# One copy of turned weights, zero rows under the query remainders, and leading parts first behind the norms

## The chip, the core and the metric

The kernel runs on one core of a Trainium2 chip. The metric is the device time of one launch in microseconds; before the change its median over three runs is 1998.62 us (1998.11 to 2001.07). The engines are named as in the profile: PE is TensorE (PEld its weight loads), DVE is VectorE, ACT is ScalarE, POOL is GpSimd, SP is SyncE, which issues the loads of weights.

## What is computed

Three transformer blocks over 512 tokens of width 1024, in float32 accuracy. The first has windowed attention (12 heads, 128 keys to either side, one learned sink logit per head), the second neighbourhood attention on a grid of 8 columns, both beside four heads that attend to 256 memory rows, and both with a gated MLP. The third has two attentions side by side, a dilated one (12 heads) and a stick-breaking one (8 heads), and an MLP with a squared ReLU. Every block begins with an RMS norm. What matters here:

```
h = rms_norm(x, g);  proj = h @ w                 # at each block and before each MLP
p = softmax(concat([q k^T / 8 + bias, sink]));  o = p[:, :keys] @ v
z = q k^T / 8
log_a = log_sigmoid(z) + suffix_sum(log_sigmoid(-z))   # stick-breaking, strictly causal
o_b = where(causal, exp(log_a), 0) @ v
```

## The kernel before

Activations lie turned: a tensor `[128, 8, 512]` holds 8 chunks of 128 features by 512 tokens. To keep float32 accuracy at the fast matmul rate, every weight and activation is split in a leading part (`w_hi`, `h_hi`, rounded) and a remainder (`w_lo`, `h_lo`), and each product is three matmuls of 128 rows and 512 columns: leading by leading, leading weight by remainder of the activation, remainder of the weight by leading activation. ACT makes the leading parts (L542 for weights, `lead`, L588, for activations), DVE the remainders (L943, and `trail`, L965). Weights come in units of 512 KB into a ring of four; a load waits until the unit four before it is used up.

The order on each engine is written out by hand, and all hand-overs are semaphores.

**The norms.** Behind each attention and each MLP of the first two blocks stands `add_normed` on DVE: for each chunk `scale` (times the norm's root, L977 or L979), `add` (into `xT`, L990), and `trail`. ACT turns each new chunk of `xT` into `h_hi`. The order is scale 0, add 0, and then per chunk scale c+1, trail c, add c+1. PE meanwhile runs `keep_busy` (3 and 16 idle matmuls) and then the first three tiles of the next stage in "stairs": `first_chunks` for chunk 0, and then per chunk c all three matmuls of tile 0, of tile 1, and of tile 2 at chunk c-2, after waiting for the remainder `h_lo` of chunk c. The stage `proj[0]` at the very start of the kernel has the same stairs, behind 12 warm-up matmuls.

**The softmax stages.** `softmax` runs over steps, each a pair of heads (on partition rows 0 to 63 and 64 to 127) and 128 queries: phase 0 has 24 window steps and 8 memory steps, phase 1 has 24 grid and 8 memory steps, phase 2 is the dilated attention. In iteration s PE makes the scores of step s (L1562), multiplies the values of step s-3 (L1602) and turns the weights of step s-2 (L1629). DVE adds the bias and finds the maximum of s (L1040) and divides step s-1 by its sum (L1062); ACT copies the turned weights of s-2 from PSUM (`copy_turned`, L653, one copy for each head), takes the exponentials of s (L665) and copies a finished pair's output (L676), whose remainder DVE takes at the end of the same iteration (L1073). In phase 0 each step also has a matmul of one column of zeros for each head (L1569), which leaves a zero in PSUM to which the sink is added as a bias.

**The stick-breaking stage.** For each head PE makes scores z into three PSUM banks (leading by leading, with the key's remainder in the other 64 rows, L1769; then the query's remainder over 64 rows, L1771; then a mask, L1777), the first half of a gate tile (L1424), the triangular sums of the head before (L1793, L1800) and the gate tile's second half. Every second head the values of a pair follow the scores (L1752). DVE reads the gate tile from its bank (L1246) before the next may start in it.

Of the kernel before, what the change touches and what calls it, by code (L numbers as in the profile page):

```python
# [8 lines left out]
P = 128  # L9
D = 1024  # L10
S = 512
DC = D // P
HD = 64
MEM = 256
# [25 lines left out]
def program(nc, t, out):  # L40
# [49 lines left out]
    with ExitStack() as ctx:  # L90
# [186 lines left out]
        class Step:  # L277


            def __init__(self, pair, pair_no, qtile, pieces, vs, biased, blocks=None, key_rows=None):  # L280
# [3 lines left out]
                self.width = sum(both[0]["width"] for both in pieces)  # L284
                self.blocks = blocks or [(first, P) for first in range(0, pieces[0][0]["keys"], P)]
# [3 lines left out]
                for p in pieces[0]:  # L289
                    if "scores" not in p:  # L290
                        p["scores"] = [(slice(0, P), p["first_key"], p["keys"], p["q"], p["k"])]
# [4 lines left out]
        def mem_steps(layer):  # L296
            steps = []
            for c in range(2):
                for i in range(4):
                    both = [dict(q=q_buf[rows(half), 6 + c, P * i:P * i + P], k=mk[rows(half), layer, c, :],  # L300
                                 bias=zero_bias[:, :], width=MEM, keys=MEM, first_key=0, sink=None, at=0)
# [6 lines left out]
        def window_steps():  # L308
            steps = []
            for c in range(6):  # L310
                for i in range(4):
                    lo_t, hi_t = max(0, i - 1), min(3, i + 1)
                    keys = P * (hi_t - lo_t + 1)
                    if hi_t == i + 1:
                        b0, first_key, sink = 1 + P * (lo_t - i + 1), 0, keys
                    else:
                        b0, first_key, sink = 0, 1, 0
                    both, vs = [], []
                    for half in range(2):
# [4 lines left out]
                                         first_key=first_key, sink=sink, at=0))  # L324
# [4 lines left out]
        def grid_steps():  # L329
# [5 lines left out]
            for c in range(6):  # L335
                for i, (k0, keys, b0, blocks, tiles, key_rows) in enumerate(spans):
                    both = [dict(q=q_buf[rows(half), c, P * i:P * i + P], k=k_buf[rows(half), c, k0:k0 + keys],
                                 bias=bias_grid[:, 2 * (c % 2) + half, b0:b0 + keys], width=keys, keys=keys,
                                 first_key=0, sink=None, at=0) for half in range(2)]
# [5 lines left out]
        def dilated_steps():  # L345

            steps = []
            for p in range(2):
                for i in range(4):
# [5 lines left out]
                    for half in range(2):  # L355
# [5 lines left out]
                        for g in (1, 2):  # L361
                            c = 2 * g + p
                            for r in range(4):
# [7 lines left out]
                                         keys=width, first_key=0, sink=None, at=0))  # L371
# [158 lines left out]
        def _(act):  # L530
# [115 lines left out]
            def copy_turned(phase, d, steps):  # L646
                if d >= 2:
                    act.wait_ge(pv_done, pv[0] + d - 1)
                for half in range(2):
# [58 lines left out]
            for c in range(DC):  # L708
                if c < 3:
                    hi_to(c)  # L710
# [223 lines left out]
        def _(dve):  # L934
# [33 lines left out]
            def add_normed(n, f, at_, f_side, post, pre, turned_layer=None):  # L968
# [44 lines left out]
            def softmax(phase, o_hi, o_lo, beside=None, read=None, last_values=None):  # L1013
                steps = attention[phase]
                n = len(steps)
                if last_values:
                    lo_to(last_values[0] + 3)
                for s in range(n + S_LAG_V):
                    if s == 2 and last_values:
                        values([last_values])  # L1020
                    if s < n:
                        st = steps[s]
                        if s >= 3:
                            dve.wait_ge(t_ready, turned[0] + sum(2 * len(x.pieces) for x in steps[:s - 2]))
                        for k, both in enumerate(st.pieces):
                            for half, p in enumerate(both):
# [9 lines left out]
                                if k:  # L1036
# [5 lines left out]
                                    in0=bank_in(phase, masked[0] % 4)[:, :p["width"]], in1=p["bias"], scale=-1.0,  # L1042
# [20 lines left out]
                    d = s - S_LAG_V  # L1063
                    if 0 <= d < n and steps[d].last:
                        st = steps[d]
                        o_count[0] += 1
                        dve.wait_ge(o_hi_done, o_count[0])
                        dst, src = o_lo[:, st.pair, :], bank_in(phase, 6 + st.pair_no % 2)[:, :]
                        lead = o_hi[:, st.pair, :].bitcast(F32)
                        if phase == 2:  # L1070
                            lead = unclassed(lead, src)[0]
                            dst, src = unclassed(dst, src)
                        nc.vector.tensor_tensor(dst, src, lead, ALU.subtract).then_inc(o_ready, 1)  # L1073
# [4 lines left out]
                turned[0] += sum(2 * len(x.pieces) for x in steps)  # L1078
# [8 lines left out]
            for c in range(DC):  # L1087
                if c < 3:
                    lo_to(c)
                trail(c, xT[:, c, :], h_hi[:, c, :], h_lo[:, c, :], G_MIX_PRE)  # L1090
# [115 lines left out]
            nc.vector.tensor_copy(ident_r[:, :], ident[:, :]).then_inc(masks_rounded, 1)  # L1206
            softmax(2, o2_hi, o2_lo, proj_sb, read_qk(range(4), lambda k: sb_q[k] if k < 4 else sb_k[k - 4]))
# [98 lines left out]
        def _(pe):  # L1306
# [29 lines left out]
            def chunk_order(st):  # L1336
# [7 lines left out]
                stairs = []  # L1344
                for c in range(1, DC):
                    stairs += [(0, 0, c), (1, 0, c)]
                    if c >= 2:
                        stairs += [(2, 0, c - 2)]
                return stairs + [(2, 0, DC - 2), (2, 0, DC - 1)] + [(k, 0, c) for k in range(3, len(st.tiles)) for c in range(DC)]

            def first_chunks(st, rhs, wait_rhs):

                (u0, _, _), (u1, _, _) = st.tiles[0][0], st.tiles[1][0]
                hi, lo = rhs(0)
                acc0, acc1 = bank_of(st, side[0], 0)[:, :], bank_of(st, side[0], 1)[:, :]
                cols = slice(0, P)
                pe.wait_ge(h_hi_done, n_h[0] - DC + 1)
                pe.wait_ge(w_hi_done, u0 + 1)
                mm(acc0, w_hi[:, u0 % 4, cols], hi, start=True, stop=False)
                pe.wait_ge(w_split, u0 + 1)  # L1360
                mm(acc0, w_lo[:, u0 % 4, cols], hi, start=False, stop=False)
                if u0 == 0:
                    wait_rhs(0)
                    mm(acc0, w_hi[:, u0 % 4, cols], lo, start=False, stop=False)
# [607 lines left out]
```

## Time and profile before

| | |
|---|---|
| median of three runs | 1998.62 us |
| the profiled execution | 2001.56 us, span 1999.8 us |
| PE busy | 1961.0 us (98%) |
| DVE busy | 964.6 us (48%) |
| ACT busy | 784.9 us (39%) |
| mean granted clock of PE | 0.994 |

The span runs from the first to the last instruction of the profiled execution; its own time is 1.76 us more. A busy share of PE of 98% says that PE hardly ever stood still, not that each matmul ran as fast as it can: the time between the starts of neighbouring matmuls is what tells that.

### The profile page before, as it was taken

The page shows a single profiled execution, that of the slowest core. Times are in us where ns is not written, and L with a number is a line of the kernel's source. Part 1 is how long each engine was busy: PE and PEld are TensorE (multiplying, and loading weights), DVE is VectorE, ACT ScalarE, POOL GpSimd, SP SyncE. Part 2 cuts the span into 40 slices and gives each one's busy share as a digit, 9 for nine tenths or more (in the row PEclk, how much of TensorE's full clock was granted, in tenths as well). Part 3 has the DMA queues.
Part 4 walks back from the last instruction along what each step waited for, and adds up shares of the span by engine and source line. Part 5 has one row for each costly group of instructions (what it writes and reads, how often), then busy time and mean ns, then how long its engine had stood idle before and what let it go on. Part 6 is the DMA issues. An engine that isn't in the chain of part 4 may idle for free.

```text
span 1999.8 us, 24785 instructions
## 1 busy us (share of the span) xinstructions
PE 1961.0 (98%) x10258; PEld 1594.3 (80%) x10258; DVE 964.6 (48%) x1461; ACT 784.9 (39%) x1315; POOL 163.7 (8%) x182
## 2 busy tenths in 40 slices
PE   9999999999999999999999999999999999999997
PEld 7976788888887866788888887988777888888886
DVE  4675465554226365465554227343554556424532
ACT  5376433333323276533333324233763443212321
POOL 3110210000004030220000002000000010000000
PEclk9999999999999999999999999999999999999999
DMA  5420233333332320233333333331202333333322
GB/s 179 140 65 24 62 115 95 95 97 97 96 100 91 95 62 24 64 106 101 99 95 92 97 99 104 95 107 49 69 30 66 106 95 96 101 99 95 95 95 84
DMA packets 51975, 178.75 MB, mean 89 GB/s; under 512 B 6364, under 2 KB 7772, under 8 KB 51736
## 3 DMA queue, kind: packets, MB, share of 16 engines
q1 hardware_dynamic: 49512, 169.14, 27.3%
q0 software_dynamic: 2208, 7.97, 1.5%
q8 instruction: 82, 1.34, 0.3%
q14 instruction: 29, 0.24, 0.0%
q10 hardware_dynamic: 144, 0.06, 0.0%
HBM read 174.48 MB, written 2.66 MB: 89 GB/s over the span
## 4 chain that ended last, share of the span: by engine, by line
PE 92%; ACT 3%; DVE 3%; issue 1%; DMA 1%; SPq 0%; DVEq 0%; ACTq 0%
PE bank L1405 24%; PE bank L1407 24%; PE bank L1406 24%; PE bank L1602 2%; PE bank L1629 2%; PE bank L1424 2%; PE bank L1562 2%; PE bank L1426 1%; PE bank L1425 1%; PE bank L1465 1%; PE bank L1464 1%; PE bank L1463 1%; ACT prob_short L665 1%; ACT pt_short L653 1%; PE bank L1793 1%
## 5 line engine op out<-in xcount | busy, mean ns | idle before, releaser
L943 DVE TENSOR_TENSOR w_lo<-w_raw,w_hi 128x1024 fp32r<-128x1024 f32 (+1 forms) x326 | 401.1, 1232 | 747.1 <-ACT w_hi L542 746.9
L1405 PE MATMUL bank<-h_hi,w_hi 128*128 128x512 f32 x1402 | 553.9, 395 | 6.6 <-DVE h_lo L965 6.4
L542 ACT CAST w_hi<-w_raw 128x1024 fp32r<-128x1024 f32 (+1 forms) x326 | 329.4, 1011 | 588.2 <-DMA w_raw<-in_w_down 133.1
L1406 PE MATMUL bank<-h_lo,w_hi 128*128 128x512 f32 x1402 | 547.0, 390 | 0.0
L1407 PE MATMUL bank<-h_hi,w_lo 128*128 128x512 f32 x1402 | 547.0, 390 | 0.0
L1405 PEld LDWEIGHTS bank<-h_hi,w_hi 128*128 128x128 f32 x1402 | 263.8, 188 | 73.2 <-DVE h_lo L965 15.8
L1407 PEld LDWEIGHTS bank<-h_hi,w_lo 128*128 128x128 f32 x1402 | 263.9, 188 | 55.7
L1406 PEld LDWEIGHTS bank<-h_lo,w_hi 128*128 128x128 f32 x1402 | 263.9, 188 | 55.4 <-issue 1.9
L1405 PE MATMUL bank<-a_hi,w_hi 128*128 128x512 f32 (+1 forms) x752 | 290.6, 386 | 0.0
L1407 PE MATMUL bank<-a_hi,w_lo 128*128 128x512 f32 (+1 forms) x752 | 289.2, 385 | 0.0
L1406 PE MATMUL bank<-a_lo,w_hi 128*128 128x512 f32 (+1 forms) x752 | 289.1, 385 | 0.0
L1405 PEld LDWEIGHTS bank<-a_hi,w_hi 128*128 128x128 f32 x752 | 141.3, 188 | 29.0 <-issue 0.9
L1406 PEld LDWEIGHTS bank<-a_lo,w_hi 128*128 128x128 f32 x752 | 141.3, 188 | 28.8 <-issue 0.7
L1407 PEld LDWEIGHTS bank<-a_hi,w_lo 128*128 128x128 f32 x752 | 141.3, 188 | 28.1
L446 POOL COPY sq_sum<-sq 128x512 f32<-128x512 f32 x6 | 3.8, 626 | 1099.7 <-ACT sq L584 1099.7
L665 ACT ACTIVATE prob_short<-prob_short,low_stat 128x256 f32<-128x256 f32 (+6 forms) x144 | 74.9, 527 | 24.1 <-DVE low_stat L1040 24.1
L759 ACT CAST a_hi<-raw 128x512 fp32r<-128x512 f32 x44 | 27.3, 621 | 125.6 <-DVE raw L1140 125.6
L449 POOL TENSOR_TENSOR sq_sum<-sq_sum,sq 128x512 f32<-128x512 f32 x36 | 49.9, 1385 | 282.4 <-ACT sq L584 282.4
L756 ACT ACTIVATE act_out<-act_out 128x512 f32<-128x512 f32 x44 | 27.8, 633 | 95.0 <-DVE act_out L1135 95.0
L1629 PE MATMUL bank<-ident,prob_short 128*128 128x128 f32 (+3 forms) x340 | 52.5, 283 | 6.7 <-DVE prob_short L1062 5.5
L653 ACT ACTIVATE pt_short<-bank 128x256 f32<-128x256 f32 (+1 forms) x128 | 44.9, 405 | 28.0 <-PE bank L1629 28.0
L1424 PE MATMUL bank<-h_hi,w_hi 128*128 128x512 f32 x128 | 53.2, 416 | 2.0 <-DVE gate_sb L1246 1.1
(219 smaller groups left out, 2213.8 us busy)
## 6 DMA issues: line engine op xcount, KB each, us to landing
w_raw<-in_w_gu SPq DMA_DIRECT2D x88, 512.0 KB, 3.5
w_raw<-in_w_mlp_in SPq DMA_DIRECT2D x32, 512.0 KB, 3.5
w_raw<-in_w_mlp_out SPq DMA_DIRECT2D x32, 512.0 KB, 3.6
w_raw<-in_w_down SPq DMA_DIRECT2D x32, 448.0 KB, 3.3
w_raw<-in_w_out SPq DMA_DIRECT2D x24, 512.0 KB, 3.6
w_raw<-in_w_down SPq DMA_DIRECT2D x16, 512.0 KB, 3.5
w_raw<-in_w_gates SPq DMA_DIRECT2D x16, 512.0 KB, 3.5
w_raw<-in_w_qk_b SPq DMA_DIRECT2D x14, 512.0 KB, 3.5
```

Source lines behind the costliest of these rows:

```text
L449: made = nc.gpsimd.tensor_tensor(sq_sum[:, :], sq_sum[:, :], sq[:, c % 2, :], ALU.add)
L542: nc.scalar.copy(slot(w_hi, v), slot(w_raw, v)).then_inc(w_hi_done, 1)
L653: nc.scalar.activation(buf[:, :w], bank_in(phase, 4 + turned[0] % 2)[:, :w], ACT.Copy).then_inc(pt_copied, 1)
L665: nc.scalar.activation(part, part, ACT.Exp, bias=top, scale=-1.0, accum_out=sums[:, s % 4, half, k:k + 1]).then_inc(p_exp, 1)
L943: nc.vector.tensor_tensor(slot(w_lo, v), slot(w_raw, v), slot(w_hi, v).bitcast(F32), ALU.subtract).then_inc(w_split, 1)
L1405: mm(acc, w1, hi, start=start, stop=False)
L1406: mm(acc, w1, lo, start=False, stop=False)
L1407: last = mm(acc, w2, hi, start=False, stop=end)
L1424: mm(ps[7][:, :], w1, hi, start=c == 0, stop=False)
L1562: last = mm(bank_in(phase, (scored[0] + half) % 4)[of, first:first + w], q, k, start=True, stop=True)
L1602: last = mm(out_, v, turned_p, start=x == 0, stop=x == n_v - 1, skip_group_check=phase == 2)
L1629: last = nc.tensor.transpose(bank_in(phase, 4 + turned[0] % 2)[:w, P * kt:P * kt + P], prob_of(phase, d, half)[:, at_ + first:at_ + first ...
```

## The change

1. Window steps keep the scores where the bias has its columns (`col`), so that the sink's zero stays in one of two fixed columns of each score bank. Eight matmuls of one column of zeros ahead of phase 0 write those columns once; the two in every step go.
2. Steps with two blocks of keys (in phase 0 the first and last query tile of a pair and all memory steps, in phase 1 all steps) turn both heads' weights into one PSUM bank, and ACT makes one copy of 512 columns in place of two of 256. Steps with three blocks and phase 2 keep two copies.
3. In phases 0 and 1 DVE takes an output's remainder one iteration later, between the maximum of step s and the division of step s-1.
4. Behind the norms DVE goes scale 0, add 0, scale 1, add 1, and then per chunk trail c, scale c+2, add c+2. PE first multiplies the leading activation of chunk c (tiles 0 and 1), then all of tile 2 at chunk c-2, and only then waits for `h_lo` of chunk c. `keep_busy` has 14 matmuls for 16. At the start of the kernel there are 16 warm-up matmuls for 12, and the second and third weight unit are split one chunk of activations later.
5. The query's remainder of the stick-breaking scores is multiplied over 128 rows, the other 64 of which DVE has set to zero ahead of phase 2.

```diff
+                if steps[d].copies == 1:
+                    both = pt_short[:, 2 * (d % 2):2 * (d % 2) + 2, :2 * P]
+                    act.wait_ge(t_ready, turned[0] + 1)
+                    nc.scalar.activation(both, bank_in(phase, 4 + turned[0] % 2)[:, :].rearrange("p (h q) -> p h q", h=2),
+                                         ACT.Copy).then_inc(pt_copied, 1)
...
-                if c < 3:
-                    hi_to(c)
+                if c in (0, 2, 3):
+                    hi_to(max(0, c - 1))
...
-                scale(0)
-                add(0)
+                for c in range(2):
+                    scale(c)
+                    add(c)
                 for c in range(DC):
-                    if c + 1 < DC:
-                        scale(c + 1)
                     trail(c, xT[:, c, :], h_hi[:, c, :], h_lo[:, c, :], pre)
-                    if c + 1 < DC:
-                        add(c + 1)
+                    if c + 2 < DC:
+                        scale(c + 2)
+                        add(c + 2)
...
+                    if phase < 2:
+                        output_remainder(s - S_LAG_V - 1)
...
+            for half in range(2):
+                none = zero_bias[rows(1 - half), :].rearrange("p (o t) -> p o t", o=1).to_broadcast([HD, 2, MEM])
+                nc.vector.tensor_copy(sb_ql[rows(1 - half), half, :].rearrange("p (o t) -> p o t", o=2),
+                                      none).then_inc(masks_rounded, 1)
...
+                for c in range(done, DC):
+                    pe.wait_ge(h_hi_done, n_h[0] - DC + c + 1)
+                    lead_part(0, c)
+                    lead_part(1, c)
+                    if c >= 2 and c - 2 >= (1 if done else 0):
+                        whole(2, c - 2)
+                    wait_rhs(c)
+                    remainder(0, c)
+                    remainder(1, c)
+                whole(2, DC - 2)
+                whole(2, DC - 1)
...
+                for bank in range(4 if phase == 0 else 0):
+                    for c in (0, 385):
+                        mm(bank_in(0, bank)[:, c:c + 1], q_buf[rows(bank % 2), 0, :P], zero_bias[rows(bank % 2), 0:1], start=True,
+                           stop=True)
...
-                            for half, p in enumerate(both):
-                                if p["sink"] is not None:
-
-                                    mm(bank_in(phase, (scored[0] + half) % 4)[:, p["sink"]:p["sink"] + 1], p["q"],
-                                       zero_bias[rows(half), 0:1], start=True, stop=True).then_inc(s_ready, 1)
...
+                            one, base = steps[d].copies == 1, 2 * P * half if steps[d].copies == 1 else 0
...
-                            last.then_inc(t_ready, 1)
-                            turned[0] += 1
+                            if half or not one:
+                                last.then_inc(t_ready, 1)
+                                turned[0] += 1
...
-                    keep_busy(16, after)
+                    keep_busy(14, after)
...
-                            mm(acc, sb_ks[own, s % 2, keys], sb_ql[own, s % 2, P * kt:], start=False, stop=False,
+                            mm(acc, sb_ks[:, s % 2, keys], sb_ql[:, s % 2, P * kt:], start=False, stop=False,
```

`lead_part` is the two matmuls by `h_hi`, `remainder` the one by `h_lo`, `whole` both. At the kernel's start chunks 0 and 1 of tiles 0 and 1 and chunk 0 of tile 2 come ahead of this loop.

## Rows read from the trace of the kernel before

**Rows 1.** Page, part 4: the chain that ended last, shares of the span

```profile
PE 92%; ACT 3%; DVE 3%; issue 1%; DMA 1%; SPq 0%; DVEq 0%; ACTq 0%
```

**Rows 2.** Waits of PE's weight loads: us in total, times, longest us

```profile
PEld bank L1602 <- ACT pt_short L653: 18.1, 44, 1.0
PEld bank L1405 <- DVE h_lo L965: 15.8, 29, 1.5
```

**Rows 3.** Timeline of a head's stick-breaking scores: start us, us, engine, line, instruction

```profile
1434.50 0.39 PE L1769 MATMUL bank<-sb_qs,sb_ks 128*128 128x512 f32 x1
1434.82 0.50 PE L1771 MATMUL bank<-sb_ql,sb_ks 64*128 64x512 f32 x1
1435.24 0.33 PE L1777 MATMUL bank<-unseen,ident_r 128*128 128x128 f32 x1
...
1437.52 0.45 PE L1424 MATMUL bank<-h_hi,w_hi 128*128 128x512 f32 x1
```

**Rows 4.** Timeline of the triangular sums, full rows throughout

```profile
1429.23 0.39 PE L1793 MATMUL bank<-L_lo,neg_tri 128*128 128x512 f32 x1
1429.46 0.34 PE L1800 MATMUL bank<-L_hi,neg_ones 128*128 128x384 f32 x1
...
1429.81 0.28 PE L1800 MATMUL bank<-L_hi,neg_ones 128*128 128x256 f32 x1
...
1430.05 0.22 PE L1800 MATMUL bank<-L_hi,neg_ones 128*128 128x128 f32 x1
```

**Rows 5.** The gate tile's bank: two timeline rows, and 8 us with clock behind POOL

```profile
1424.75 0.77 PE L1424 MATMUL bank<-h_hi,w_hi 128*128 128x512 f32 x1 [1.05 <-DVE gate_sb L1246]
...
1435.39 0.69 DVE L1246 TENSOR_TENSOR gate_sb<-bank,rstd 128x512 f32<-128x512 f32 x1
...
1420.00:1428.00 8.00, 6.95 (x23) 4.75 (x22) 7.56 (x10) 7.30 (x12) 0.00 (x0) 0.79 0.22 66
```

**Rows 6.** Timeline behind the first norm of block one, DVE and PE

```profile
229.45 0.69 DVE L977 TENSOR_TENSOR f_in_big<-f_in_big,rstd 128x512 f32<-128x512 f32 x1 [3.73 <-ACT rstd L600]
230.18 0.69 DVE L990 TENSOR_TENSOR xT<-xT,f_in_big 128x512 f32<-128x512 f32 x1
230.79 0.68 DVE L977 TENSOR_TENSOR f_in_big<-f_in_big,rstd 128x512 f32<-128x512 f32 x1
...
231.66 0.75 DVE L965 SCALAR_TENSOR_TENSOR h_lo<-xT,gains,h_hi 128x512 fp32r<-128x512 f32 x1 [0.19 <-ACT h_hi L588]
...
231.88 0.47 PE L1359 MATMUL bank<-h_hi,w_hi 128*128 128x512 f32 x1
...
232.33 0.69 DVE L990 TENSOR_TENSOR xT<-xT,f_in_big 128x512 f32<-128x512 f32 x1
...
246.69 0.91 DVE L965 SCALAR_TENSOR_TENSOR h_lo<-xT,gains,h_hi 128x512 fp32r<-128x512 f32 x1 [0.80 <-ACT h_hi L588]
...
251.22 0.39 PE L1405 MATMUL bank<-h_hi,w_hi 128*128 128x512 f32 x1
```

**Rows 7.** Timeline of softmax steps: window, grid, and dilated (the last row)

```profile
127.34 0.28 PE L1569 MATMUL bank<-zero_bias,q_buf 64*128 64x1 f32 x4
127.55 0.66 PE L1602 MATMUL bank<-pt_short,v_buf 128*64 128x128 f32 x8
...
133.00 0.88 PE L1629 MATMUL bank<-ident,prob_short 128*128 128x128 f32 x6 [0.30 <-DVE prob_short L1062]
...
733.56 0.66 PE L1629 MATMUL bank<-ident,prob_short 128*128 128x128 f32 x4
...
734.10 0.66 ACT L653 ACTIVATE pt_short<-bank 128x256 f32<-128x256 f32 x2 [0.33 <-PE bank L1629]
...
734.81 0.81 PE L1602 MATMUL bank<-pt_short,v_buf 128*64 128x128 f32 x8
...
1389.44 1.08 ACT L653 ACTIVATE pt_dil<-bank 128x512 f32<-128x512 f32 x2 [5.25 <-PE bank L1629]
```

**Rows 8.** Timeline at the start of the kernel, PE

```profile
13.22 0.79 PE L1405 MATMUL bank<-h_hi,w_hi 128*128 128x512 f32 x1
```

More of the change, by code:

```diff
@@ L290, in __init__ @@
                     if "scores" not in p:
-                        p["scores"] = [(slice(0, P), p["first_key"], p["keys"], p["q"], p["k"])]
+                        self.copies = 1 if len(self.blocks) == 2 else 2
+                        p["scores"] = [(slice(0, P), p["col"] + p["first_key"], p["keys"], p["q"], p["k"])]
         def rows(half):
@@ L313, in window_steps @@
                     keys = P * (hi_t - lo_t + 1)
[L314 to L317, printed above, removed]
+                    b0, first_key = (1 + P, 0) if i == 0 else (0, 1)
                     both, vs = [], []
@@ L338, in grid_steps @@
                                  bias=bias_grid[:, 2 * (c % 2) + half, b0:b0 + keys], width=keys, keys=keys,
-                                 first_key=0, sink=None, at=0) for half in range(2)]
+                                 first_key=0, col=0, at=0) for half in range(2)]
                     vs = [[v_buf[part, kt, P * c + 64 * half:P * c + 64 * half + 64]
@@ L1017, in softmax, with output_remainder @@
                     lo_to(last_values[0] + 3)
+                def output_remainder(d):
+                    if not (0 <= d < n and steps[d].last):
+                        return
+                    st = steps[d]
+                    o_count[0] += 1
+                    dve.wait_ge(o_hi_done, o_count[0])
+                    dst, src = o_lo[:, st.pair, :], bank_in(phase, 6 + st.pair_no % 2)[:, :]
+                    lead = o_hi[:, st.pair, :].bitcast(F32)
+                    if phase == 2:
+                        lead = unclassed(lead, src)[0]
+                        dst, src = unclassed(dst, src)
+                    nc.vector.tensor_tensor(dst, src, lead, ALU.subtract).then_inc(o_ready, 1)
                 for s in range(n + S_LAG_V):
@@ L1023, in softmax @@
                         if s >= 3:
-                            dve.wait_ge(t_ready, turned[0] + sum(2 * len(x.pieces) for x in steps[:s - 2]))
+                            dve.wait_ge(t_ready, turned[0] + sum(x.copies for x in steps[:s - 2]))
                         for k, both in enumerate(st.pieces):
@@ L1041, in softmax @@
                                     out=prob_of(phase, s, half)[:, p["at"]:p["at"] + p["width"]],
[L1042 removed]
+                                    in0=bank_in(phase, masked[0] % 4)[:, p["col"]:p["col"] + p["width"]], in1=p["bias"], scale=-1.0,
                                     scalar=start, op0=ALU.add, op1=ALU.min,
@@ L1062, in softmax @@
                             nc.vector.tensor_scalar(part, part, rden[:, i, half:half + 1], None, ALU.mult).then_inc(p_ready, 1)
[L1063 to L1073, printed above, removed]
+                    if phase == 2:
+                        output_remainder(s - S_LAG_V)
                     if beside and s < len(beside.tiles) + 1:
@@ L1077, in softmax @@
                         read(s, ps[7], beside.after(s))
-                turned[0] += sum(2 * len(x.pieces) for x in steps)
+                if phase < 2:
+                    output_remainder(n - 1)
+                turned[0] += sum(x.copies for x in steps)
             masked, expd, dens, rdens, o_count, turned = [0], [0], [0], [0], [0], [0]
@@ L1657, in _ @@
             pe.wait_ge(ones_set, 1)
-            for _ in range(12):
+            for _ in range(16):
                 mm(ps[7][:, :P], ones[:, :], ones[:, :], start=True, stop=True)
@@ L1759, in _ @@
                     z = [ps[3 * (s % 2) + b] for b in range(3)]
-                    own = rows(s % 2)
                     if s >= 2:
```

78 lines of the change are left out of this document (42 added, 36 removed).

## The prediction

> **What bounds the kernel now.** First the chain that ended last: 92% of it is PE [rows 1], and PE is busy for nearly the whole span. So a microsecond is won only where PE either waits or issues its matmuls further apart than it could. Next the waits of PE's weight loads: the two largest sums are for ACT's copies of turned weights, 18.1 us in 44 waits, and for `h_lo` behind the norms, 15.8 us in 29 [rows 2]. They are upper bounds, since a load that waits may do so under a running matmul. Last the timeline, for the distances between starts of matmuls, where the page sees nothing: a stretch can be 100% busy and still be slack. All parts of the change touch one of these three, and each is costed in its own stage. Signs: minus is faster.
>
> **Stick-breaking scores.** A head's scores take 1437.52 - 1434.50 = 3.02 us from first start to the next tile [rows 3]. Around the 64-row matmul the starts are 0.32 and 0.42 us apart. Where all matmuls have 128 rows, 512 columns follow each other after 0.23 us, 384 after 0.175 (two in 0.35), 256 after 0.12 (two in 0.24), and for 128 I take half of that, 0.06 [rows 4]. The scores of a head are two each of 512, 384, 256 and 128 columns and masks of 128, 256 and 128: 0.46 + 0.35 + 0.24 + 0.12 + 0.24 = 1.41 us. Saved at full effect 1.61 us a head.
>
> Who is late next? The next gate tile needs its bank read by DVE: that read ended at 1435.39 + 0.69 = 1436.08, while the tile would now start at 1434.50 + 1.41 = 1435.91 [rows 3, 5]. It hangs on the triangular sums before it, so it does not move along; with the hand-over PE waits 0.22. On heads 3, 5 and 7 the values of a pair (over 2 us) stand between and hide this: 3 x 1.61 = 4.83. On heads 2, 4 and 6: 3 x 1.39 = 4.17. On heads 0 and 1 nothing is won: PE already waits 1.05 us for the first bank [rows 5], and that read ends a chain over ACT and DVE (rounding of head 1, absolute values, exponentials, logarithms, split) which does not begin earlier; 3.2 us more of waiting swallow both savings. Sum -9.0.
>
> That longer stand has a price. After the 1.05 us the clock fell to the lower of its two levels, 1.2 GHz, and the 8 us around it show a mean of 0.79 [rows 5], so 0.42 x 8 = 3.4 us at 1.2 GHz (1 is 2.4 GHz, and 0.5 is 1.2 GHz), in part while PE stood. With 4.3 us of standing, more of the slow time falls on matmuls: at most all 3.4 us, which costs 1.7, against about 1.0 now. +0.7, and up to +3 if a second such stretch follows. The Trainium skill (TensorE: Matmul & The Clock Gate, "HAM oscillation — how this bites in real kernels") says that a PE left waiting between bursts is put back to half rate and pays again for warming up. By that rule, too, the stand is not free; it changes none of the terms.
>
> The two DVE writes of zeros come before phase 2, where DVE is idle; a 128x512 pass of such kind is 0.69 [rows 6], so 1.4 us at worst, taken as 0.
>
> **Norms, four times.** Before, DVE's loop is add, ACT's leading part, trail, next add: from the first trail to the eighth (246.69 - 231.66)/7 = 2.15 us a chunk [rows 6]. The eighth ends at 247.60, and then PE still has 15 matmuls: tiles 0, 1 and 2 of the stair's end. The next tile starts at 251.22, 21.77 us after the first scale [rows 6].
>
> After: a dependent add follows its scale after 0.73, an independent instruction an add after 0.61, and a trail is followed after 0.67 [rows 6]. The loop is 0.67 + 0.73 + 0.61 = 2.01 a chunk (2.06 where scale reads PSUM), free of ACT. The first trail starts at 2 x 1.34 = 2.68, the eighth, with nothing but the seventh in front, at about 15.6, and ends at 16.5 with its 0.91. PE has 72 matmuls of 0.23: 16.6 us. It can begin at 2.2 (the first `h_hi`; now 231.88 - 229.45 = 2.43, in part `keep_busy`, whose two matmuls less give that 0.2), waits about 0.3 and 0.6 for the first two remainders, and restarts cost 0.1 each; then nothing stops it: 2.2 + 16.6 + 1.1 = 19.9, or 20.0. Against 21.77: -1.75 a norm. Bounds: PE never waits, 18.8, is -2.9; if DVE keeps its 2.15 a chunk and all trails come 0.7 later, the eighth ends near 18.9, and eight matmuls (1.84) end at 20.8: -0.95. Four norms: -7.0 (-11.6 to -3.8). Behind the stair, weights of its fifth tile are ready early enough: their load hangs on tile 0's end, which moves by some 0.8, and the tile starts 5.5 us after the stair, so little is lost.
>
> **Start of the kernel.** At 13.22 PE has 12 of the stair's 72 matmuls behind it [rows 8]. In the new order it can have 15 by then, since chunk 1 no longer stands behind the second unit's split: 3 x 0.23 = 0.7, and 0.6 for waits of the later chunks and slow clock. The warm-up's four more end about when the first real matmul can start. -1.3 (-2.5 to +0.5).
>
> **Softmax, phases 0 and 1.** In the grid a turn starts at 733.56, ACT's two copies at 734.10, they last 0.66, and the values start at 734.81: 1.25 us, and PE waits for the copy [rows 7]. With one copy ACT may start only when the second head is turned too, two transposes later (0.29), and a 512-column copy lasts 0.60 (two take 1.08 [rows 7], the second starting 0.49 behind the first): 0.54 + 0.29 + 0.60 + 0.05 = 1.48. So the edit that frees ACT lengthens PE's loop: +0.22 a step that has no other wait. Against it, every four steps DVE no longer waits for ACT's output copy; that wait held the turn at 133.00, idle 0.30 and 0.06 of start-up [rows 7], about 0.6 where steps are short.
> - Grid: 6 pairs x (4 x 0.22 - 0.6) = +1.7; memory steps 2 x 0.28 = +0.3 after rounding down for the last. +2.0.
> - Window: the group of zeros costs 127.55 - 127.34 = 0.21 [rows 7], but a switch from 64 to 128 rows then stays exposed for about 0.10. A pair of heads: the step of 256 keys that turned in 1.33 now needs 1.48, and with ACT's queue behind it the next is 0.27 later in all; the other one-copy step wins 0.07, the three-block step 0.16, the wait gone 0.36: -0.35 a pair, -2.1, and +0.5 for the memory steps: -1.6.
> - Eight zero matmuls once (4 x 0.21 = 0.84, partly under a wait that is there) and longer copies in the tails: +0.5.
> Together +0.9. Bounds: if the single copy costs nothing, 52 steps lose no 0.22 and it is about -9; if each of the 52 is late by 0.4, it is +10.
>
> **Sum.** -9.0 + 0.7 - 7.0 - 1.3 + 0.9 = -15.7. The profiled execution took 2001.56 (span 1999.8), 2.9 above the median; its own time would become 1985.9. Taken from the median of the three runs: 1998.6 - 15.7 = 1982.9, say 1983.
>
> **Rivals.**
> A. Rows do not matter: the distances of 0.32 and 0.42 come from something else. The Trainium skill (same page, "Why this matters for your kernels") says that a single matmul over few rows takes the time of a full one, and (under "The mechanism") that a weight load runs ahead only if its row group differs. By that rule zero rows buy nothing. As a mechanism here: PE keeps 3.02 us a head, the -9.0 and the +0.7 go: 1991.2. Against it: full rows follow at 0.23 under their own loads [rows 4], and only next to 64 rows the load stands bare [rows 3]. 5%.
> B. The single copy is not on PE's loop, as the exponentials are what is late; DVE's wait goes all the same. Softmax gives -9 instead of +0.9: 1973. The wait of 44 loads on ACT [rows 2] speaks against it. 8%.
> C. The norms give only their lower bound and the start nothing: +3.2 + 1.3: 1987.4. DVE and POOL share time there (0.91 for a trail of 0.75 [rows 6]). 12%.
> D. Slower than before: ACT's single copy, queued behind exponentials, starts so late that each of the 52 steps loses 0.22 + 15.7/52 = 0.52 us or more. From there on the time is above 1998.6; at 0.6 it is 2003. The dilated copies of the same width speak against it [rows 7]. 2%.
> The forecast itself 71%, with 1978 to 1988 as its own range. The remaining 2%: something undoes it all within 0.2%.
>
> **How the numbers follow.** About 0.2% (4 us) is what a measurement can tell from no change. A, B and C are all faster by more. Faster 0.96, same 0.02, slower 0.02. The range takes in C and most of A and B: 1974 to 1991.
>
> **What would show it.** Right: heads 3, 5, 7 of the stick stage shorter by 1.6 and 2, 4, 6 by 1.4, with a short wait for L1246; a stand of some 4 us ahead of head 1's tile; from first scale to fourth tile 20.0 us; turn to values 1.48 in the grid, and no turn waiting for DVE. Wrong: score starts still 0.4 apart, a slow clock over many heads, a grid period well off 8.5 us.

## The result, and the profile after

The changed kernel takes 1981.51 us (median of 4 runs, 1980.01 to 1982.82), the kernel before 1999.39 us beside it: ratio 0.9908, 95% interval 0.9892 to 0.9924, 17.9 us faster. The forecast was 1983 us, 15.7 us faster. The profiled execution of after took 1981.45 us with a span of 1979.7 us, 20.1 us less than that of before.

The chain that ended last is PE for 92%, as in [rows 1]; what moved is inside it. The chain's shares, and then the waits (us in total, times, longest), PE's weight loads first and PE's matmuls last:

```profile
PE 92%; ACT 3%; DVE 2%; DMA 1%; issue 1%; SPq 0%; DVEq 0%; ACTq 0%
```

```profile
PEld bank L1638 <- ACT pt_short L651: 26.7, 48, 1.0
PEld bank L1638 <- ACT pt_short L659: 7.3, 12, 0.7
...
PEld bank L1380 <- DVE h_lo L971: 4.8, 9, 0.8
...
PE bank L1461 <- DVE gate_sb L1265: 5.2, 3, 4.0
```

Against [rows 2]: the wait behind the norms fell from 15.8 to 4.8. The wait for ACT's copies grew from 18.1 to 34.0: 26.7 where one copy serves both heads (L651) and 7.3 where there are two (L659). The gate tile's bank is new among the large ones.

Where the 20.1 us went is read from the starts of ACT's `rstd` (at both ends of each norm's stairs) and, in block three, of DVE's `gate_sb` reads. Each column is how many us longer a stretch is than in the kernel before, in one profiled execution of each kernel; "norms" is the sum of four. The kernels below the first are those of the experiments.

```
kernel              start  window  norms   grid  block three    all
after               -1.46   -2.26  -7.19  +0.12    -9.31      -20.1
stick_rows          +0.72   -0.02  +0.05  -0.11    -8.69       -8.1
norms_only          -1.56   -0.02  -7.20  -0.15    -0.27       -9.2
norm_order_pe       -1.52    0.00  -3.81  -0.12    -3.14       -8.6
norm_order_dve      +0.91   -0.06  -1.87  -0.05    -3.11       -4.2
one_copy_only       -0.11   +1.80  +0.06  +3.67    -2.00       +3.4
moved_remainder     -0.34   -2.70  +0.01  -3.75    -3.13       -9.9
two_copies          -1.87   -3.87  -7.15  -3.54    -8.86      -25.3
gate_read_first     -1.73   -2.20  -7.19  +0.33   -14.23      -25.0
values_lag_4        -1.45   -5.44  -7.19  -3.02   -10.46      -27.6
lag_4_two_copies    -1.51   -5.71  -7.23  -3.66    -9.09      -27.2
all_waits           -1.37   -5.97  -7.11  -6.05   -15.92      -36.4
no_late_remainder   -1.66   -5.59  -7.13  -3.77   -15.96      -34.1

block three         to head 0   head 1   heads 2-7   slow clock in head 7
after                 -1.63      +1.09     -7.10          -1.67
stick_rows             0.00      +0.11     -7.13          -1.67
norms_only            -0.02      +1.32     +0.04          -1.67
norm_order_pe         -0.05      -1.42      0.00          -1.67
moved_remainder       -1.61      +0.07     +0.04          -1.67
one_copy_only         -1.62      +1.28      0.00          -1.67
```

The lower table splits block three by the `gate_sb` reads ("to head 0" is from the last norm to the first of them) and tells clock from mechanism. The rows below are windows of 8 us with PE's granted clock in the third column from the end (1 is 2.4 GHz), first of before, then of after at the same work:

```profile
1240.00:1248.00 8.00, 8.00 (x39) 7.08 (x38) 8.00 (x15) 6.13 (x7) 0.00 (x0) 0.93 0.22 66
1248.00:1256.00 8.00, 8.00 (x32) 6.46 (x31) 3.05 (x4) 1.88 (x2) 0.00 (x0) 0.86 0.21 66
1496.00:1504.00 8.00, 8.00 (x32) 4.08 (x32) 2.53 (x5) 5.40 (x9) 0.00 (x0) 0.79 0.11 33
```

```profile
1232.00:1240.00 8.00, 8.00 (x41) 7.08 (x40) 7.45 (x10) 3.32 (x5) 0.00 (x0) 1.00 0.22 59
...
1480.00:1488.00 8.00, 8.00 (x50) 6.10 (x50) 1.62 (x3) 5.66 (x10) 0.00 (x0) 1.00 0.12 35
```

Two stretches at 1.2 GHz are gone, behind the last norm and in head 7, worth 1.63 and 1.67 us. They aren't counted as the change's doing, since one_copy_only, whose part touches neither place, loses both as well. With head 1's +1.09, which is clock too, that is 2.2 us of the profile's 20.1, which leaves 17.9 for the mechanisms and the start of the kernel; that it equals the difference of the medians is chance.

**Stick-breaking scores**, head 2 in after, the head of [rows 3] (timeline: start us, us, engine, line, instruction):

```profile
1423.15 0.39 PE L1806 MATMUL bank<-sb_qs,sb_ks 128*128 128x512 f32 x1
1423.38 0.39 PE L1808 MATMUL bank<-sb_ql,sb_ks 128*128 128x512 f32 x1
1423.61 0.22 PE L1814 MATMUL bank<-unseen,ident_r 128*128 128x128 f32 x1
...
1424.88 0.47 PE L1461 MATMUL bank<-h_hi,w_hi 128*128 128x512 f32 x1
```

Starts are 0.23 apart where they were 0.32 and 0.42, and first score to tile is 1.73 us for 3.02. The weight load of the query's remainder tells why, first of before, then of after:

```profile
1434.81 0.18 PEld L1771 LDWEIGHTS bank<-sb_ql,sb_ks 64*128 64x128 f32 x1 [0.35 <-issue]
```

```profile
1423.16 0.19 PEld L1808 LDWEIGHTS bank<-sb_ql,sb_ks 128*128 128x128 f32 x1
```

Over 64 rows the load began 0.31 us behind the start of the matmul ahead of it, just before its own matmul. Over 128 rows it begins 0.01 behind, and lies wholly under the running matmul. Ahead of head 1's tile PE now stands for 3.95 us, which answers to [rows 5]; DVE, PE, and one window:

```profile
1407.81 1.49 DVE L1255 TENSOR_TENSOR L_lo<-prob,L_hi 128x1280 fp32r<-128x1280 f32 x1
1409.22 2.35 DVE L949 TENSOR_TENSOR w_lo<-w_raw,w_hi 128x1024 fp32r<-128x1024 f32 x2
1411.49 0.69 DVE L1265 TENSOR_TENSOR gate_sb<-bank,rstd 128x512 f32<-128x512 f32 x1
...
1412.32 0.76 PE L1461 MATMUL bank<-h_hi,w_hi 128*128 128x512 f32 x1 [3.95 <-DVE gate_sb L1265]
...
1408.00:1416.00 8.00, 4.05 (x13) 3.16 (x12) 7.07 (x9) 6.66 (x11) 0.00 (x0) 0.68 0.17 61
```

**A norm**, the one of [rows 6]:

```profile
225.73 0.69 DVE L983 TENSOR_TENSOR f_in_big<-f_in_big,rstd 128x512 f32<-128x512 f32 x1 [3.80 <-ACT rstd L599]
...
228.39 0.75 DVE L971 SCALAR_TENSOR_TENSOR h_lo<-xT,gains,h_hi 128x512 fp32r<-128x512 f32 x1
...
240.58 2.66 DVE L971 SCALAR_TENSOR_TENSOR h_lo<-xT,gains,h_hi 128x512 fp32r<-128x512 f32 x2
...
245.53 0.50 PE L1442 MATMUL bank<-h_hi,w_hi 128*128 128x512 f32 x1
```

First scale to fourth tile is 245.53 - 225.73 = 19.80 us for 21.77, and from the first trail to the seventh (240.58 - 228.39)/6 = 2.03 a chunk for 2.15. **The grid**, which answers to [rows 7]; turn, copy, values:

```profile
751.19 0.66 PE L1666 MATMUL bank<-ident,prob_short 128*128 128x128 f32 x4
...
751.94 0.60 ACT L651 ACTIVATE pt_short<-bank 128x512 f32<-128x512 f32 x1 [0.52 <-PE bank L1666]
...
752.59 0.80 PE L1638 MATMUL bank<-pt_short,v_buf 128*64 128x128 f32 x8
```

Turn to values 1.40 us, where it was 1.25; by the starts of the turns a pair of heads takes 8.26 us in the grid (8.27 before) and 9.12 in the window (9.57).

### The profile page after: what moved, and what is told of

It is laid out like the page before. It is cut to its first block, busy times and chain, and to the rows that moved or that the text cites. A ratio compares the mean times of both kernels' runs of the same rounds, so it can differ in the third digit from the quotient of the medians.

```text
span 1979.7 us, 24575 instructions
## 1 busy us (share of the span) xinstructions
PE 1941.9 (98%) x10178; PEld 1583.6 (80%) x10178; DVE 970.5 (49%) x1463; ACT 779.7 (39%) x1263; POOL 160.9 (8%) x182
## 4 chain that ended last, share of the span: by engine, by line
PE 92%; ACT 3%; DVE 2%; DMA 1%; issue 1%; SPq 0%; DVEq 0%; ACTq 0%
PE bank L1442 23%; PE bank L1443 23%; PE bank L1444 23%; PE bank L1638 3%; PE bank L1666 2%; PE bank L1461 2%; ACT pt_short L651 1%; PE bank L1502 1%; PE bank L1501 1%; PE bank L1500 1%; PE bank L1462 1%; PE bank L1463 1%; PE bank L1380 1%; PE bank L1375 1%; PE bank L1372 1%; PE bank L1603 1%
## 5 line engine op out<-in xcount | busy, mean ns | idle before, releaser
L1442 PE MATMUL bank<-h_hi,w_hi 128*128 128x512 f32 x1292 | 507.4, 393 | 0.2 <-DVE q_buf L1015 0.2
L1444 PE MATMUL bank<-h_hi,w_lo 128*128 128x512 f32 x1292 | 502.8, 389 | 0.0
L1443 PE MATMUL bank<-h_lo,w_hi 128*128 128x512 f32 x1292 | 502.7, 389 | 0.0
L1442 PEld LDWEIGHTS bank<-h_hi,w_hi 128*128 128x128 f32 x1292 | 242.6, 188 | 54.9 <-issue 2.8
L1443 PEld LDWEIGHTS bank<-h_lo,w_hi 128*128 128x128 f32 x1292 | 242.6, 188 | 51.6 <-issue 1.9
L1444 PEld LDWEIGHTS bank<-h_hi,w_lo 128*128 128x128 f32 x1292 | 242.5, 188 | 50.7
L765 ACT CAST a_hi<-raw 128x512 fp32r<-128x512 f32 x44 | 27.3, 621 | 125.5 <-DVE raw L1154 125.5
L1461 PE MATMUL bank<-h_hi,w_hi 128*128 128x512 f32 x128 | 53.5, 418 | 6.1 <-DVE gate_sb L1265 5.2
L923 ACT CAST a_hi<-raw 128x512 fp32r<-128x512 f32 x32 | 19.9, 621 | 83.9 <-DVE raw L1303 83.9
```

The lines of the kernel that those rows point to most:

```text
L765: nc.scalar.copy(a_hi[:, pair, :], raw[:, p, :]).then_inc(a_hi_done, 1)
L1442: mm(acc, w1, hi, start=start, stop=False)
L1443: mm(acc, w1, lo, start=False, stop=False)
L1444: last = mm(acc, w2, hi, start=False, stop=end)
L1461: mm(ps[7][:, :], w1, hi, start=c == 0, stop=False)
```

## The experiments

Medians are in us with the kernel before beside them; the intervals are those of the ratio.

**stick_rows**: part 5 alone.

```diff
-mm(acc, sb_ks[own, s % 2, keys], sb_ql[own, s % 2, P * kt:], ...)
+mm(acc, sb_ks[:, s % 2, keys], sb_ql[:, s % 2, P * kt:], ...)   # other rows set to zero
```

> The kernel before with nothing but part 5 of the change: the query's remainder over 128 rows, half of them zeros. Theory (rows matter: a 64-row matmul between full rows leaves a weight load bare): heads 2 and 4, 6 of the stick-breaking stage shorter by 1.3 and 0.7 us, heads 3, 5, 7 by 1.4, nothing on heads 0 and 1, and the longer stand ahead of head 1's gate tile gives back about 1 us in slow clock; in all 6 us less than before (1.3 + 1.4 + 1.4 + 0.7 + 0.7 + 1.4 - 1.1 = 5.8). Rival A (rows do not matter): the scores keep their 0.32 and 0.42 us, 0 us. Rival on the clock: the slow stretches near 1247 us and near 1499 us of the kernel before, 1.7 us each, depend on what stands around them; if this part alone takes the second away, 7.5 us.

1993.82 against 2000.72, ratio 0.9964 (0.9951 to 0.9977): 6.9 faster. The scores' starts are those of after, with the rest of the kernel as it was, so rival A falls. Of the 8.1 us of its profile 7.13 are in heads 2 to 7; the slow clock at the start cost 0.72 more, and that in head 7 is gone:

```profile
1435.22 0.39 PE L1772 MATMUL bank<-sb_qs,sb_ks 128*128 128x512 f32 x1
1435.45 0.39 PE L1774 MATMUL bank<-sb_ql,sb_ks 128*128 128x512 f32 x1
1435.68 0.22 PE L1780 MATMUL bank<-unseen,ident_r 128*128 128x128 f32 x1
1435.74 0.39 PE L1772 MATMUL bank<-sb_qs,sb_ks 128*128 128x384 f32 x1
1435.96 0.34 PE L1774 MATMUL bank<-sb_ql,sb_ks 128*128 128x384 f32 x1
```

**norms_only**: part 4 alone, the diff as under "The change".

> The kernel before with nothing but part 4: two scales and adds ahead of the first trail, PE's leading parts first, 14 for 16 idle matmuls, and the start of the kernel with 16 warm-up matmuls and units split one chunk later. Theory: 4 x 1.8 = 7.2 us at the norms and 1.5 at the start, 8.7 us in all, and a first scale to fourth tile of 20.0 us. Rival C: the trails are what is late, whatever the order of PE, 3.8 us at the norms and 0 at the start. Rival on the clock: 1.7 us more, if the slow stretch near 1247 us goes with this part, since that stretch lies behind the last norm.

1992.32, ratio 0.9956 (0.9941 to 0.9971): 8.4 faster. In the profile 7.20 of it is at the norms and 1.56 at the start; rival C falls.

**norm_order_pe** and **norm_order_dve**: the halves of it.

```diff
 # norm_order_pe: PE as after, DVE as before
+lead_part(0, c); lead_part(1, c); whole(2, c - 2); wait_rhs(c); remainder(0, c); remainder(1, c)
 # norm_order_dve: DVE as after, PE as before
+scale(0); add(0); scale(1); add(1); then per chunk trail(c), scale(c + 2), add(c + 2)
```

> The kernel before with PE's order alone of part 4 (leading parts and the third tile ahead of the wait for the remainder, 14 idle matmuls, and all of the start of the kernel); DVE keeps scale, trail, add. Theory (DVE's loop is what paces the stairs, 2.15 us a chunk held by ACT's leading part; PE's order only decides how much is left at the end): the eighth trail stays at 18.2 us behind the first scale, and only two remainders and two tiles' last chunks, 8 matmuls, are left behind it: about 1 us a norm, so 4 us at the norms and 1.5 at the start. Rival (PE's order is the whole of it): 7.2 and 1.5.

> The kernel before with DVE's order alone of part 4 (two scales and adds ahead of the first trail); PE keeps its stairs. Theory (PE waits for the first trail, which is now 1.3 us later, before it does anything with it, but the eighth trail ends 1.6 us earlier): with 15 matmuls left behind the eighth trail PE gains 1.6 us less what it stood at the start, between 0 and 1.6 us a norm, 3 us in all. Rival (DVE's order is the whole of it): 7.2 us. Rival (alone it delays the first remainder and loses): 2 us slower.

1994.49 (0.9974, 0.9965 to 0.9984) and 1997.33 (0.9987, 0.9977 to 0.9996) against 2000.40. In the profiles they give 0.95 and 0.47 per norm; together they give 1.80, more than the sum. With PE's order alone the trails keep their old pace, and PE starts the fourth tile 20.77 us after the first scale:

```profile
227.93 0.69 DVE L977 TENSOR_TENSOR f_in_big<-f_in_big,rstd 128x512 f32<-128x512 f32 x1 [3.82 <-ACT rstd L600]
...
245.17 0.91 DVE L965 SCALAR_TENSOR_TENSOR h_lo<-xT,gains,h_hi 128x512 fp32r<-128x512 f32 x1 [0.79 <-ACT h_hi L588]
...
248.70 0.39 PE L1423 MATMUL bank<-h_hi,w_hi 128*128 128x512 f32 x1
```

The eighth trail starts 17.24 us after the first scale, as in [rows 6]. The size came as expected, the reason only in part: the trail ends at 246.08 and PE is still at leading parts, which it had waited for. PE's waits in these stairs, of norm_order_pe and then of norm_order_dve:

```profile
PE bank L1353 <- ACT h_hi L588: 1.4, 3, 0.6
```

```profile
PE bank L1405 <- DVE h_lo L965: 1.6, 2, 1.3
```

With PE's order alone it waits for ACT, whose leading parts come at DVE's old pace; with DVE's order alone it waits for the first trails. After has 0.6 and 0.3 us of the two. So each order takes away the wait that the other leaves, and is worth its full amount only with it.

**one_copy_only**: part 2 alone.

```diff
-for half in range(2): nc.scalar.activation(buf[:, :w], bank[:, :w], ACT.Copy)
+nc.scalar.activation(both, bank[:, :].rearrange("p (h q) -> p h q", h=2), ACT.Copy)
```

> The kernel before with nothing but part 2, one copy of 512 columns for both heads. Theory (the copy is on PE's loop): turn to values grows from 1.25 to 1.41 us in the 52 steps that have it, so 52 x 0.16 = 8 us slower than before, less where another wait covers it: 4 to 9 us slower. Rival B (the copy is not on PE's loop): the same time as before. A rival of the other sign: ACT is freed by 0.06 us a step and its exponentials come earlier: 1 to 3 us faster.

2005.35 against 2000.72, ratio 1.0025 (1.0016 to 1.0035): 4.6 slower. **moved_remainder**: part 3 alone.

```diff
+output_remainder(s - S_LAG_V - 1)   # between maximum of s and division of s-1
-output remainder of s - S_LAG_V at the end of the iteration
```

> The kernel before with nothing but part 3, DVE's remainder of a pair's output one iteration later. Theory (DVE waits for ACT's output copy every fourth step and holds up the turn): a pair of heads is shorter by 0.4 us in the window (9.57 to about 9.2) and by 0.5 in the grid (8.27 to about 7.75), 16 pairs with the memory steps, so 5 to 8 us faster. Rival: the copy's latency sets PE's loop also in that step, so that DVE's wait has cover: within 1 us of before.

1991.65, ratio 0.9954 (0.9937 to 0.9970): 9.1 faster, above the 5 to 8 expected. In the profile, which says 9.9, 6.5 is in the two softmax stages, inside that range, and 3.1 is slow stretches that are missing in block three. Turns of the grid, one copy alone first; the bracket is PE's wait for DVE in every fourth step:

```profile
733.88 0.70 PE L1639 MATMUL bank<-ident,prob_short 128*128 128x128 f32 x4 [0.40 <-DVE prob_short L1071]
...
742.65 0.70 PE L1639 MATMUL bank<-ident,prob_short 128*128 128x128 f32 x4 [0.40 <-DVE prob_short L1071]
```

```profile
724.17 0.65 PE L1637 MATMUL bank<-ident,prob_short 128*128 128x128 f32 x4
...
731.91 0.66 PE L1637 MATMUL bank<-ident,prob_short 128*128 128x128 f32 x4
```

A pair takes 742.65 - 733.88 = 8.77 us with the copy alone, 731.91 - 724.17 = 7.74 with the moved remainder alone, 8.27 before and 8.26 after: +0.50 and -0.53, which cancel. This is where the grid's gain went.

**two_copies**: after with part 2 undone.

```diff
-self.copies = 1 if len(self.blocks) == 2 else 2
+self.copies = 2
```

> The kernel after, with two copies of 256 columns again in every step (part 2 undone, the rest of the change kept). Theory (the single copy lengthens PE's loop): turn to values falls from 1.41 to 1.25 us in 52 steps, 5 to 9 us faster than the kernel after, about 1975 us; the grid's pair of heads falls from 8.26 to about 7.7 us. Rival (with the remainder moved, two copies load ACT so that the exponentials are late): within 2 us of the kernel after, the turn then waiting for DVE's division.

1976.51 against 2000.92, ratio 0.9881 (0.9867 to 0.9896), 5.0 below the kernel after (timed apart). The grid's pair is 7.72 us for 8.26, and window and grid together are 5.3 us shorter than in after. The two ratios' intervals overlap by 0.0004, so the stages and one_copy_only, whose interval excludes 1, carry the verdict: part 2 costs, also where the other parts are in. The sum of waits for ACT's copies would not have told it: it is 27.9 us here, for 18.1 before, in a faster kernel, while the loads' wait for DVE's division fell from 9.1 to 3.7.

**gate_read_first**: after, with DVE's read ahead of the split.

```diff
-lo_to(gates_sb.after(s) + 2)
 dve.wait_ge(unit_done, gates_sb.after(s))
 nc.vector.tensor_tensor(gate_sb[:, s, :], ps[7][:, :], rstd[:, :], ALU.mult).then_inc(acc_read_dve, 1)
+lo_to(gates_sb.after(s) + 2)
```

> The kernel after, with DVE's read of the gate tile's bank put ahead of the split of a weight unit in each head of the stick-breaking stage. Theory (that read stands in DVE's queue behind the split, not behind its own data): the stand of 3.95 us ahead of head 1's tile falls by the 2.3 us of the two splits, the waits of 0.6 us on heads 4 and 6 go, and half a microsecond of slow clock with them: 3 to 5 us faster than the kernel after, about 1977.5 us. Rival (the split is then late, and the tile behind it waits for its weights instead): within 1 us of the kernel after.

1976.53, ratio 0.9883 (0.9869 to 0.9898): 5.0 below after; the two ratios' intervals overlap by 0.0006, so this verdict too rests on the stages. The stand ahead of head 1 falls from 3.95 to 1.68 us, and the window around it, with that stand in it, is at full clock:

```profile
1410.83 0.68 DVE L1264 TENSOR_TENSOR gate_sb<-bank,rstd 128x512 f32<-128x512 f32 x1
1411.43 2.35 DVE L949 TENSOR_TENSOR w_lo<-w_raw,w_hi 128x1024 fp32r<-128x1024 f32 x2
...
1411.65 0.47 PE L1461 MATMUL bank<-h_hi,w_hi 128*128 128x512 f32 x1 [1.68 <-DVE gate_sb L1264]
...
1408.00:1416.00 8.00, 6.32 (x35) 5.46 (x34) 7.87 (x11) 7.89 (x13) 0.00 (x0) 1.00 0.21 68
```

Block three is 4.9 us shorter than in after (14.23 against 9.31). Clock has two shares in it: after loses 2.5 us in head 1 (12.56 us between the gate reads, for 10.05 in norm_order_pe at full clock), and this kernel has the 1.63 behind the last norm. That leaves about 4.0 us for the moved read.

**values_lag_4** and **lag_4_two_copies**: after, with one step more between copy and values, and the same with two copies.

```diff
-S_LAG_T, S_LAG_V = 2, 3
+S_LAG_T, LAGS = 2, (4, 4, 3)     # by phase
```

> The kernel after, with the values of a step multiplied one step later in phases 0 and 1 (step s-4 for s-3), so that a whole step lies between ACT's copy and PE's use of it. Theory (PE waits 0.3 us in each step for the copy and for nothing else): PE's waits for turned weights, 26.7 us by the profile, go, and the loop becomes that of DVE, some 1.85 us a step for 2.07 in the grid: 8 to 14 us faster, about 1970 us. Rival (DVE's or ACT's loop is as long as PE's already): the waits only change their name, within 2 us of the kernel after.

> As the run with the values one step later, and with two copies in every step. Theory (the copy has left PE's loop, ACT has not enough work to matter): the same time as with one copy within 1 us, so that the sign of part 2 hangs on the lag alone. Rival (ACT is the next bound once PE doesn't wait): the 0.06 us a step that two copies cost more show, 2 to 5 us slower than with one copy.

1974.85 (0.9876, 0.9859 to 0.9892) and 1974.77 (0.9872, 0.9857 to 0.9887). The first is 6.7 below after, less than the 8 to 14 expected. Two of its waits:

```profile
PEld bank L1666 <- DVE prob_short L1083: 8.4, 23, 1.1
...
PEld bank L1638 <- ACT pt_short L651: 2.7, 5, 0.5
```

ACT's single copy is named for 2.7 us (26.7 in after), but DVE's division, 2.7 us there, is 8.4 here. That DVE's loop is next is read from this wait alone. With the lag, one copy or two makes no difference to the medians (0.1 us) and 0.9 us in the two stages, for 5.0 and 5.3 without it. So part 2's cost is, by these runs, the latency of the copy inside PE's loop.

**all_waits** and **no_late_remainder**: lag, two copies and early gate reads together; the first also has DVE's output remainder behind the division.

```diff
+if s == 0: read_gate(s)              # ahead of L_hi; for s > 0 ahead of lo_to
-output_remainder(s - lag_v - 1)      # ahead of the division
+output_remainder(s - lag_v - 1)      # behind it (all_waits only)
```

> The kernel after, with the values one step later and two copies in phases 0 and 1, DVE's remainder of a pair's output behind the division instead of ahead of it, the gate tile's bank read ahead of the split of a weight unit, and for head 0 ahead of the rounding too. Theory (each removes a wait of PE that nothing else covers): 6.7 for the lag, 5.0 for the read, 1.6 for head 0 (the stand of 1.68 us that was left), and about 2 for the remainder (0.7 us of DVE waiting in each pair, a part of it on the loop): 15 us faster than the kernel after, about 1966 us. Rival (the moved remainder delays DVE's maximum of the next step instead, and gives nothing): 1968 us.

> As the run before it, with DVE's remainder left between maximum and division. Theory: 2 us slower than that run, about 1968 us. Rival: the same time, since PE's loop hides what DVE waits.

1965.02 (1963.45 to 1965.17), ratio 0.9827 (0.9813 to 0.9840), and 1966.71, ratio 0.9837 (0.9824 to 0.9850), against 2000.40. The first beats both kernels: 35.4 below before, 16.5 below after. The late remainder's own 1.7 us was expected as 2 and lies in the grid (6.05 against 3.77), but the two intervals overlap. DVE in all_waits now reads head 0's gate bank ahead of the rounding, and the chain is PE for 96%:

```profile
1398.79 0.69 DVE L1240 TENSOR_TENSOR gate_sb<-bank,rstd 128x512 f32<-128x512 f32 x1
1399.40 0.82 DVE L1257 CAST L_hi<-prob 128x1280 fp32r<-128x1280 f32 x1
```

```profile
PE 96%; DVE 2%; ACT 1%; DMA 1%; issue 0%; SPq 0%; DVEq 0%; ACTq 0%
```

## Why the prediction was right

The forecast missed the median by 1.5 us, and that closeness is in part luck. In the profiles the steps come to -20.1 for -15.7: 3.3 of the difference is the two slow stretches, and the largest errors of the steps, +1.9 and -3.0, have opposite signs. By its steps, predicted against measured in the profiles:

**Norms, -7.0 against -7.19.** The loop of 2.01 to 2.06 a chunk is there (2.03), and first scale to fourth tile is 19.80 for 20.0. Two steps were wrong without harm. PE begins 2.42 us behind the first scale (228.15 - 225.73), as before, and not at 2.2: it waits 0.6 for the first `h_hi`, so two idle matmuls fewer give nothing here; of the two waits for remainders only one, of 0.3, is there. And the eighth trail was to end at 16.5 us and ends near 17.5. It starts at 15.7, as forecast, but lasts 1.79 where 0.91 was counted (1.79 to 1.81 in the other three norms). POOL's sum of squares begins 0.05 ahead of it; that this is the cause was not tested. PE reaches it just then, after 64 of its 72 matmuls, and doesn't stop. The two order experiments show that the gain belongs to both halves.

**Start, -1.3 against -1.46.** At 13.22 us, the time of [rows 8], the kernel after has 15 matmuls behind it, as forecast (the sixteenth starts at 13.23). But how much of that is the new order is not shown, because the clock differs too. First of before, then of after:

```profile
8.00:16.00 8.00, 6.24 (x19) 4.25 (x19) 5.19 (x6) 7.13 (x12) 0.00 (x0) 0.79 1.03 409
```

```profile
8.00:16.00 8.00, 6.54 (x26) 4.57 (x27) 5.21 (x7) 7.25 (x12) 0.00 (x0) 1.00 1.02 406
```

The same window is at full clock in all nine kernels with the new start and below it (0.57 or 0.79) in all five with the old one, among them stick_rows and norm_order_dve, which for this reason show +0.72 and +0.91. A clock of 0.79 over 8 us costs up to 1.7 us, as much as the whole gain. Warm-up matmuls, order and later splits weren't run apart, so which of them keeps the clock up stays open.

The sixteenth matmul of after:

```profile
13.23 0.40 PE L1372 MATMUL bank<-h_hi,w_hi 128*128 128x512 f32 x1
```

**Stick-breaking, -9.0 against -7.1 (heads 2 to 7).** That rows matter was right, and the saving on heads 0 and 1 is nothing, as forecast (head 1's tile starts 12.43 us earlier, as much as head 0's first score). What failed is in the question who is late next: head 2's wait was taken over for heads 4 and 6. The gate tile's bank read does hang on the triangular sums, but through DVE's queue, where the rounding `L_hi`, its remainder `L_lo` and the split of a weight unit that nobody waits for yet stand ahead of it. On heads 4 and 6 the remainder of a pair's output stands there too, which the row of head 2 in [rows 5] does not have. Head 4 of after:

```profile
1445.26 0.69 DVE L1260 TENSOR_TENSOR a_lo<-bank,a_hi 128x512 fp32r<-128x512 f32 x1
1445.86 1.22 DVE L949 TENSOR_TENSOR w_lo<-w_raw,w_hi 128x1024 fp32r<-128x1024 f32 x1
1446.99 0.69 DVE L1265 TENSOR_TENSOR gate_sb<-bank,rstd 128x512 f32<-128x512 f32 x1
...
1447.83 0.47 PE L1461 MATMUL bank<-h_hi,w_hi 128*128 128x512 f32 x1 [0.61 <-DVE gate_sb L1265]
```

So heads 4 and 6 gave 0.67 and 0.68, not 1.39 (head 2 gave 1.27). gate_read_first shows it: the read moved, and the waits went. The rest is a size: next to one of 128 columns a matmul holds PE longer than the rows of long streams said, 384 columns 0.22 and not 0.175 (stick_rows, above: 1435.74 to 1435.96 is the distance behind the 128-column mask; the kernel before has 0.23 there in its triangular sums, 1430.22 to 1430.45, a row the forecast didn't read), and a head's scores take some 0.14 more than the 1.41 counted; heads 3, 5 and 7 gave 1.49, not 1.61. The Trainium skill (TensorE: Matmul & The Clock Gate, "Why this matters for your kernels") says that a single matmul over few rows takes the time of a full one. No run here has such a matmul by itself, and for the stream the trace does not agree: stick_rows adds rows of zeros and wins 6.9 us, as the loads of 64 rows no longer stand bare.

**Clock, +0.7 against +1.09 in after.** The size was near by luck. The reason, more standing so more slow clock, isn't a rule of this kernel: norm_order_pe has the same stand as before and stays at full clock, and two_copies, with after's stand of 4.0 us, shows -0.10 in head 1, so no more slow clock there than before.

```profile
1419.25 0.47 PE L1442 MATMUL bank<-h_hi,w_hi 128*128 128x512 f32 x1 [1.04 <-DVE gate_sb L1246]
...
1416.00:1424.00 8.00, 6.96 (x35) 5.50 (x34) 6.10 (x9) 6.34 (x10) 0.00 (x0) 1.00 0.21 66
```

Two stretches elsewhere went that the forecast had left alone (1.63 and 1.67). What sets them stays open.

**Softmax, +0.9 against -2.14.** The sign of the sum was wrong: a small loss was forecast, a gain came. The mechanism was right, both ways: the single copy costs (so rival B falls; D falls by the result), the moved remainder pays. The mis-sized term is turn to values: 1.48 predicted, 1.40 measured. ACT starts 0.75 us behind the turn, not 0.83; over 52 steps 0.08 is 4 us, about what the sum is off by (3.0), if the steps with another wait don't feel it. In a pair of the grid the copy was counted as 0.88 and costs 0.50, the moved remainder was counted as 0.6 and gives 0.53. Part 1 has no run of its own; two_copies less moved_remainder leaves about 1.2 us for it in the window (3.87 - 2.70). Part 2's effect as a whole, 4.6 us slower, was forecast as the larger half of a small sum and never priced by itself against leaving it out; two_copies shows that the change would have been 5 us better without it.

## What to carry to other kernels

One operation in place of two saves the engine that issues it and costs the engine that waits for the first half: if the copy's latency lies in the bound engine's loop, price the loop, not the copy, and here a step more of lag was worth more (6.7 us) than either form of the copy. When a wait's releaser is named, look at what stood ahead of it in its queue; here a weight split that was not due held a bank read for up to 2.3 us. And parts of a change should be read stage by stage, since +0.50 and -0.53 us in one loop look like nothing happened.

## What the runs showed of the hardware

The lower clock level comes in stretches that cost 1.4 to 2.5 us, at a few places (the start, behind the last norm, head 1; the end is left out here), but not in each profile: behind the last norm 9 of 14 kernels have it, in head 7 only the kernel before, both with PE busy for the whole window. It comes and goes between kernels that are the same there, so one profile of a small part can say 3.3 us too much or too little; moved_remainder gained 6.5 us by mechanism and 9.9 in its profile. One kernel's executions differ as well: those of before range from 1996.19 us at a mean clock of 0.998 to 2001.67 at 0.994.

A 64-row matmul between full ones costs 0.32 and 0.42 us between starts, where zeros in the other rows give 0.23, and its weight load starts only with it, where a full one starts with the matmul ahead.
